# Modulation column sums take a way through DRAM and a turn more before TensorE's product

## The reference, cut to what matters

```python
cs = jax.nn.silu(c)
for i in range(DEPTH):
    ada = cs @ w_ada[i] + b_ada[i]
    sh1, sc1, g1, sh2, sc2, g2 = jnp.split(ada, 6, axis=-1)
    u = x * (1.0 + sc1) + sh1
    ...
    x = _layer_norm(DEEPNORM_ALPHA * x + (1.0 + g1) * y, ...)
```

## Time and profile before

| | |
|---|---|
| median of 3 runs | 3165.83 us (3165.27 to 3168.71) |
| profiled execution, span from first to last instruction | 3166.5 us |
| TensorE busy | 2985.3 us, 94% |
| TensorE weight loads | 2434.7 us, 77% |
| VectorE busy | 1981.5 us, 63% |
| ScalarE busy | 1090.8 us, 34% |
| GpSimd busy | 97.7 us, 3% |
| DMA | 346.08 MB, mean 109 GB/s |
| mean granted TensorE clock | 0.976 |

### The profile page before, as it was taken

The page is one execution under the profiler, slowest core; times in us unless marked ns, Lnnn a source line. Parts: engine busy times, 40 slices in busy tenths (PEclk is TensorE's granted clock), DMA queues, the critical chain, the costliest instruction groups (busy, mean ns, idle before and its releaser), DMA issues.

```text
span 3166.5 us, 45854 instructions
## 1 busy us (share of the span) xinstructions
PE 2985.3 (94%) x19638; PEld 2434.7 (77%) x19656; DVE 1981.5 (63%) x3051; ACT 1090.8 (34%) x1667; POOL 97.7 (3%) x116
## 2 busy tenths in 40 slices
PE   6998999999988999997999999899999998899999
PEld 5876888887865788884867887678887877778887
DVE  5856897787567896787455777654444255554353
ACT  2334432233156332233333333242223244542122
POOL 0000000000000000000002222000000001000000
PEclk8999999999998999998999999899999999999999
DMA  8751554545530464542210000222322220032232
GB/s 235 187 160 54 180 179 163 183 160 173 189 106 21 153 199 146 200 163 65 95 49 11 13 13 10 103 87 97 103 93 92 83 94 27 8 107 93 94 105 81
DMA packets 236543, 346.08 MB, mean 109 GB/s; under 512 B 19620, under 2 KB 121964, under 8 KB 236340
## 3 DMA queue, kind: packets, MB, share of 16 engines
q1 hardware_dynamic: 221236, 329.63, 32.3%
q10 hardware_dynamic: 15104, 13.52, 1.3%
HBM read 340.97 MB, written 2.15 MB: 108 GB/s over the span
## 4 chain that ended last, share of the span: by engine, by line
PE 80%; DVE 11%; ACT 5%; DMA 2%; issue 1%; SPq 0%; DVEq 0%; ACTq 0%
PE bank L141 79%; DVE w_tiles L150 2%; PE bank L144 2%; DVE w_low L150 1%; DMA first_ada<-in_w_ada 1%; ACT w_high L147 1%; DVE ada_acc L162 1%; DMA weight_ring<-in_d_w_in 1%; DVE w_g L150 1%; ACT w_tiles L147 1%; DVE x_natural L162 1%; ACT L147 1%; ACT stage L147 0%; DVE d_sm L168 0%; DVE x_sm L168 0%
## 5 line engine op out<-in xcount | busy, mean ns | idle before, releaser
L150 DVE TENSOR_TENSOR w_low<-weight_ring,w_high 128x2048 fp32r<-128x2048 f32 (+2 forms) x212 | 463.8, 2188 | 450.4 <-ACT w_high L147 450.4
L147 ACT ACTIVATE w_high<-weight_ring 128x2048 fp32r<-128x2048 f32 (+2 forms) x212 | 388.1, 1831 | 610.4 <-DMA weight_ring<-in_mlp_down 178.9
L141 PE MATMUL bank<-u_high,w_high 128*128 128x512 f32 x1472 | 578.4, 393 | 12.1 <-DVE w_low L150 6.2
L141 PE MATMUL bank<-u_high,w_low 128*128 128x512 f32 x1472 | 574.8, 390 | 0.0
L141 PE MATMUL bank<-u_low,w_high 128*128 128x512 f32 x1472 | 574.6, 390 | 0.0
L141 PE MATMUL bank<-w_high,u_high 128*128 128x512 f32 x896 | 353.3, 394 | 6.8 <-DVE w_low L150 2.5
L141 PE MATMUL bank<-w_low,u_high 128*128 128x512 f32 x896 | 351.1, 392 | 0.0
L141 PE MATMUL bank<-w_high,u_low 128*128 128x512 f32 x896 | 351.0, 392 | 0.0
L141 PEld LDWEIGHTS bank<-u_high,w_high 128*128 128x128 f32 x1472 | 277.5, 189 | 70.6 <-ACT stage L147 7.1
L141 PEld LDWEIGHTS bank<-u_high,w_low 128*128 128x128 f32 x1472 | 277.4, 188 | 58.7
L141 PEld LDWEIGHTS bank<-u_low,w_high 128*128 128x128 f32 x1472 | 277.7, 189 | 57.0
(11 more groups left out here) (411 smaller groups left out, 4362.5 us busy)
## 6 DMA issues: line engine op xcount, KB each, us to landing
ada_ring<-in_mod_w SPq DMA_DIRECT2D x48, 1024.0 KB, 7.5
weight_ring<-in_f_w_up SPq DMA_DIRECT2D x44, 1024.0 KB, 5.1
ada_ring<-in_w_ada SPq DMA_DIRECT2D x40, 1024.0 KB, 7.1
weight_ring<-in_mlp_up SPq DMA_DIRECT2D x32, 1024.0 KB, 5.4
weight_ring<-in_mlp_down SPq DMA_DIRECT2D x32, 1024.0 KB, 5.0
weight_ring<-in_f_w_down SPq DMA_DIRECT2D x24, 768.0 KB, 4.7
weight_ring<-in_m_w_in SPq DMA_DIRECT2D x16, 1024.0 KB, 10.2
weight_ring<-in_d_w_in SPq DMA_DIRECT2D x12, 1024.0 KB, 5.3
```

The lines of the kernel that those rows point to most:

```text
L141: return self.e.matmul(out, l, r, start=start, stop=stop, skip_group_check=True)
L147: return self.e.activation(out, in_, f, **kw) if self.live else QUIET
L150: return self.e.tensor_tensor(out, a, b, op) if self.live else QUIET
```

## The change

- VectorE's eight operations on a block stay, but the sum is made in place in `ada_ring`: the second half (s = 1) first, then the first half, whose first operation adds the sum of the second. `ada_acc` and VectorE's wait for the product before it are gone.
- SyncE sends the sum, 128 x 512 floats, to DRAM (`sp_sum_out`) in the block that follows: it issues the half s = 1, waits for the sum, stores it, waits until the store has landed, and issues the half s = 0.
- SyncE loads the sum back (`sp_sum_in`) in another order: 128 floats on each partition, four such groups side by side. In its queue this stands behind the first weight tile of the next turn.
- GpSimd adds the four groups with two additions, of 128 x 256 and 128 x 128 (`pool_sums`).
- TensorE makes one product instead of four, with the 128 x 128 sum as the stationary operand and a 128 x 4 picking matrix as the moving one, a turn later than before (`takes`); so the first turn of m_qk has none and the first turn of g0_up0 has one.
- `pick` is made once by a VectorE reduction at the start.
- The gate f0 is stored and loaded between f0_up0 and f0_dn0 (before: stored in the m cell, loaded at the start of f0). Gates d and x are stored behind dn0 instead of ahead of it, and g1 behind g0_dn0.

```diff
@@ -299,10 +300,10 @@
...
         self.small = take("small", [P, 96])
-        self.fold, self.eps = self.small[:, 64:80], self.small[:, 80:82]
+        self.fold, self.eps, self.pick = self.small[:, 64:80], self.small[:, 80:82], self.small[:, 88:92]
         self.X = take("x_natural", [P, TT, D])
         self.aring = take("ada_ring", [P, 2, 2048])
-        self.aacc = take("ada_acc", [P, 512])
+        self.asum = take("ada_sum", [P, 4, P])
         weights = -(-ar.top // 64) * 64
...
@@ -489,13 +490,16 @@
...
         at = turn = 0
-        self.ada_bank = {}
+        self.takes, summed = {}, None
         for x in lin:
...
             turn += x.turns
-            for i, b in enumerate(x.ada or ()):
-                self.ada_bank[b] = x.group(i)
+            for i, b in enumerate(x.ada):
+                if summed is not None:
+                    self.takes[x.name, i] = summed
+                summed = b
+        self.takes["g0_up0", 0] = summed
         self.lin = {x.name: x for x in lin}
...
@@ -559,6 +563,8 @@
...
             self.sp_weight(sp, w)
+            self.sp_sum_in(sp)
+        self.sp_sum_out(sp, last.ada[-1])
         sp.wait_ge(self.T, "used", last.tile(last.turns - 1, len(last.pieces) - 1))
...
@@ -634,12 +642,44 @@
...
         w = self.ada_blocks[b][0]
-        for s in range(2):
+        for s in (1, 0):
             if b > len(self.ada_first):
-                sp.wait_ge(self.V, "ada used", b - 1, s)
+                if s:
+                    sp.wait_ge(self.V, "ada used", b - 1)
+                else:
+                    self.sp_sum_out(sp, b - 1)
+                    sp.wait_ge(self.fold_out, b - 1)
             src = w[s * 512:(s + 1) * 512, :].rearrange("(k p) n -> p k n", p=P)
...
             sp.dma_start(dst, src).then_inc(*self.ada_in[s].landed(b))
+
+    def sp_sum_out(self, sp, b):
+        if b > self.stored_sum:
+            sp.wait_ge(self.V, "ada summed", b)
+            if b - 2 >= len(self.ada_first):
+                sp.wait_ge(self.fold_in, b - 2)
+            sp.dma_start(self.fold_rows[b % 2], self.aring[:, 0, 0:512]).then_inc(*self.fold_out.landed(b))
+            self.stored_sum = b
+
+    def sp_sum_in(self, sp):
+        b = self.stored_sum
+        if b > self.loaded_sum:
+            sp.wait_ge(self.fold_out, b)
+            if b > len(self.ada_first):
+                sp.wait_ge(self.T, "ada", b - 1)
+            src = self.fold_rows[b % 2].rearrange("a n -> (a n)").rearrange("(q p m) -> p q m", q=4, p=P)
+            sp.dma_start(self.asum[:], src).then_inc(*self.fold_in.landed(b))
+            self.loaded_sum = b
+
+    def pool_sums(self, g, *names):
+        for name in names:
+            for i in range(self.lin[name].turns):
+                if (name, i) in self.takes:
+                    b = self.takes[name, i]
+                    g.wait_ge(self.fold_in, b)
+                    g.tensor_tensor(self.asum[:, 0:2, :], self.asum[:, 0:2, :], self.asum[:, 2:4, :], ALU.add).then_inc(*self.G.up())
+                    g.wait_ge(self.G)
+                    g.tensor_tensor(self.asum[:, 0, :], self.asum[:, 0, :], self.asum[:, 1, :], ALU.add).then_inc(*self.G.up("folded", b))
 
...
@@ -754,43 +793,41 @@
...
                 self.T.mark("used", w)
-            if i < len(L.ada):
-                self.pe_ada(pe, L.ada[i])
+            self.pe_ada(pe, name, i)
             if between and i == 0:
...
 
-    def pe_ada(self, pe, b):
-        bank = self.ada_bank.get(b, 7)
-        pe.wait_ge(self.V, "ada summed", b)
-        if bank in self.free:
-            pe.wait_ge(*self.free[bank])
-        for j in range(4):
-            m = pe.matmul(self.bank[bank][:, j:j + 1], self.aacc[:, j * P:(j + 1) * P], self.ones[:, 0:1], True, True)
-        m.then_inc(*self.T.up("ada", b))
-        self.free[bank] = (self.V, "mod", b)
-
-    def dve_ada_take(self, v, b):
-        _, bias, at, _ = self.ada_blocks[b]
-        v.wait_ge(self.T, "ada", b)
-        v.tensor_tensor(self.mod[:, at:at + 4], self.bank[self.ada_bank.get(b, 7)][:, 0:4], bias, ALU.add).then_inc(
-            *self.V.up("mod", b))
+    def pe_ada(self, pe, name, i):
+        if (name, i) in self.takes:
+            b, bank = self.takes[name, i], self.lin[name].group(i)
+            pe.wait_ge(self.G, "folded", b)
+            if bank in self.free:
+                pe.wait_ge(*self.free[bank])
+            pe.matmul(self.bank[bank][:, 0:4], self.asum[:, 0, :], self.pick, True, True).then_inc(*self.T.up("ada", b))
+            self.free[bank] = (self.V, "mod", b)
+
+    def dve_ada_take(self, v, name, i):
+        if (name, i) in self.takes:
+            b, bank = self.takes[name, i], self.lin[name].group(i)
+            _, bias, at, _ = self.ada_blocks[b]
+            v.wait_ge(self.T, "ada", b)
+            v.tensor_tensor(self.mod[:, at:at + 4], self.bank[bank][:, 0:4], bias, ALU.add).then_inc(*self.V.up("mod", b))
 
...
         cs = self.ada_blocks[b][3]
-        for s in range(2):
+        for s in (1, 0):
             v.wait_ge(self.ada_in[s], b)
+            acc = self.aring[:, s, 0:512]
             for t in range(4):
...
                 src = self.aring[:, s, t * 512:(t + 1) * 512]
-                if s == t == 0:
-                    v.wait_ge(self.V)
-                    if b > len(self.ada_first):
-                        v.wait_ge(self.T, "ada", b - 1)
-                    v.tensor_scalar(self.aacc[:], src, col, None, ALU.mult).then_inc(*self.V.up())
+                v.wait_ge(self.V)
+                if t:
+                    v.scalar_tensor_tensor(acc, src, col, acc, ALU.mult, ALU.add).then_inc(*self.V.up())
+                elif s:
+                    v.tensor_scalar(acc, src, col, None, ALU.mult).then_inc(*self.V.up())
                 else:
-                    v.wait_ge(self.V)
-                    v.scalar_tensor_tensor(self.aacc[:], src, col, self.aacc[:], ALU.mult, ALU.add).then_inc(*self.V.up())
-            self.V.mark("ada used", b, s)
+                    v.scalar_tensor_tensor(acc, src, col, self.aring[:, 1, 0:512], ALU.mult, ALU.add).then_inc(*self.V.up("ada used", b))
         self.V.mark("ada summed", b)
...
@@ -865,8 +902,8 @@
...
                 xs, tmp = self.X[:, t, i * 512:(i + 1) * 512], self.stage[:, t % 2, :]
-                if t == TT - 1 and i < len(L.ada):
-                    self.dve_ada_take(v, L.ada[i])
+                if t == TT - 1:
+                    self.dve_ada_take(v, name, i)
                 v.wait_ge(self.T, "sum", name, i, t)
...
@@ -1162,6 +1199,8 @@
...
         self.dve_split(v, 1)
+        v.wait_ge(self.core_in, "core")
+        v.tensor_reduce(self.pick, self.ident.rearrange("p (r g) -> p g r", g=4), ALU.add).then_inc(*self.V.up("pick"))
 
...
@@ -1241,7 +1280,6 @@
...
         self.act_norm_rows(a, self.m_ln, 0)
-        self.act_gate_store(a, "f0")
         self.act_turn(a, "m o u", self.cols["m_norm_g"], None)
...
@@ -1305,6 +1342,7 @@
...
     def pool_m(self, g):
+        self.pool_sums(g, "m_qk", "m_v", "m_o")
         self.join(g, self.G, "m cell start")
...
@@ -1507,13 +1545,16 @@
...
         f, st = self.f[l], f"f{l}"
-        self.act_gate_load(a, st, f["gb"][:])
+        if l:
+            self.act_gate_load(a, st, f["gb"][:])
         self.act_norm_rows(a, f["ln"], 2 * l + 1)
...
         self.act_ffn_up(a, l, st + "_up0", 0, None)
-        for gate in (("x",) if l else ("d",)):
-            self.act_gate_store(a, gate)
+        if not l:
+            self.act_gate_store(a, "f0")
+            self.act_gate_load(a, "f0", f["gb"][:])
         self.act_residual(a, st + "_dn0")
+        self.act_gate_store(a, "x" if l else "d")
         self.act_ffn_up(a, l, st + "_up1", 6, [(st + "_up0", 10), (st + "_up0", 11)])
...
@@ -1685,6 +1726,7 @@
...
     def pool_diff(self, g):
+        self.pool_sums(g, "m_out", "f0_up0", "f0_dn0", "f0_up1", "f0_dn1", "d_qk", "d_v")
         self.join(g, self.G, "d heads start")
...
@@ -1958,7 +2000,9 @@
...
     def pool_rwkv(self, g):
+        self.pool_sums(g, "d_out", "f1_up0", "f1_dn0", "f1_up1", "f1_dn1", "r_out")
         self.pool_wkv(g)
+        self.pool_sums(g, "g0_up0")
 
...
@@ -2627,6 +2669,8 @@
...
                 self.act_residual(a, f"{st}_dn0")
+                if not l:
+                    self.act_gate_store(a, "g1")
         dn = f"{st}_dn1"
...
@@ -2658,6 +2702,7 @@
...
                         self.dve_ahead(v, up, i, b // 2)
+                self.dve_ada_take(v, up, i)
             if h == 0:
```

More of the change, by code:

```diff
@@ L230, with __init__ @@
 class Net:
-    def __init__(self, nc, ctx, args, out, scratch, gate_rows):
-        self.nc, self.a, self.out, self.scratch, self.gate_rows = nc, args, out, scratch, gate_rows
+    def __init__(self, nc, ctx, args, out, scratch, gate_rows, fold_rows):
+        self.nc, self.a, self.out, self.scratch, self.gate_rows, self.fold_rows = nc, args, out, scratch, gate_rows, fold_rows
         self.T, self.V = Signal(nc, "tensor_done"), Signal(nc, "vector_done")
@@ L515, in write @@
```

(13 more changed lines are left out.)

6 lines of the change are left out of this document (3 added, 3 removed).

## The result

The changed kernel takes 3183.0 us (median of 4 runs, 3178.6 to 3194.3) against 3165.6 us before (4 runs, 3161.7 to 3168.7). The ratio is 1.0058, with a 95% interval from 1.0044 to 1.0072: slower by 0.6%, where 3146 us was forecast. A later session gave 3178.2 us (10 runs) against 3169.0 (20 runs), a ratio of 1.0024 (1.0009 to 1.0038). The profiled execution took 3182.8 us, with a span of 3181.4 us.

The account below looks back on a forecast made before the run. The prediction took TensorE, busy 94% of the span, as the bound. Its terms, 20.5 + 4.4 - 1.6 - 2.7 + 0.4 - 0.8 = 20.2 us off 3165.8, gave 3146 us, range 3129 to 3163.

Parts of the forecast that it names:

- Term 3: SyncE's queue elsewhere: the sum's store delays weight tiles, hidden in dense turns, costing 1.6 us at the end of m_out.
- Term 2: m_o and d_v: TensorE's waits for VectorE's sums go, but later weight tiles limit the gain to 4.4 us.
- Term 5: GpSimd's additions slow VectorE by 0.1 us in each of eight VectorE-set turns, costing 0.8 us.
- Term 4: f0_dn0: gate f0's store and load delay ScalarE and VectorE, so TensorE waits 2.7 us.
- Term 1: Small products on TensorE: six of eight passes go, 0.66 us in 30 turns, 20.5 us with two first turns.
- D: Rival, 10%: sum stores land in 12 us or more, SyncE's tiles come late, dense turns stall; about 3180 us.
- B: Rival, 16%: waits for sums gain nothing, m_out loses 5 us, f0_dn0 8.7 with the clock; about 3159 us.
- E: Rival, 8%: the folded sum is late at the small product, TensorE waits for GpSimd; about 3166 us.
- C: Rival, 10%: GpSimd locks VectorE out for whole instructions in eight turns, 10.4 instead of 0.8 us; about 3155 us.

Follow-up runs that it names:

- e1: The changed kernel measured and profiled once more, with no edit: 3178.2 us.
- e7: The changed kernel with f0's gate rows stored a stage earlier, ahead of f0_up0's passes on ScalarE: 3168.9 us, ratio 0.9984.
- e2: The kernel before with one four-column small product in place of four, leaving out part of the sums; no DRAM, GpSimd or later turn: 3147.4 us, ratio 0.9918.
- e5: The changed kernel with the sum in its own tile and f0's gate rows stored a stage earlier: 3146.1 us, ratio 0.9908.
- e6: The changed kernel without GpSimd's two additions, three of four partial rows left out: 3172.3 us, ratio 0.9987.
- e11: e5 without GpSimd's two additions, three of four partial rows left out: 3139.5 us, ratio 0.9901.
- e12: The kernel before measured and profiled once more, with no edit: 3171.4 us.
- e4: The changed kernel with the sum in its own tile, so the first half loads without waiting for the store's landing: 3159.0 us, ratio 0.9969.
- e3: The kernel before with its four small products a turn later from a second accumulator, gate rows moved, no DRAM or GpSimd: 3165.0 us, ratio 0.9991.

## Why the prediction was wrong

The forecast was 3146, the result 3183, outside the range of 3129 to 3163. At r_r.0 the forecast's terms give -19.7 us and the run gave +4.4. Of these 24 us Term 3 misses 10, Term 2 9, Term 5 4 and Term 4 2, and Term 1 gave 2 more than it promised. By its own steps:

- **Term 1** held: 0.70 us a turn instead of 0.66 and 28 free turns instead of 30, 19.6 us against 19.8. The first turn of m_qk gave 2.1 (1.1 in e1). That m_qk.1 and m_qk.2 were counted among the free turns was wrong: they lost 2.7.
- **Term 2** is -5.0 us where +4.4 stood. Its chain of waits was right: the waits of the earlier trace rows went, 4.5 and 5.0 us, the tile in m_o went out 4.7 us later in its stage where I had 4, and the cell and the heads started 1.6 us sooner, counted from the start of m_o.0 and d_v.0, where 2.3 and 2.1 stood. What failed is what I left out behind it. I saw that VectorE would set the joint start while TensorE's turn got shorter, and put no price on the idle time that this opens, 6.35 and 6.23 us: a lower clock was priced only behind the gap that went away. The cell behind it took 4.4 us longer and the heads 3.8, 8.2 of the 9.4 us that this term misses. For the cell all fourteen traces bear this out, for the heads they don't (first section).
- **Term 3** had the mechanism and not the size, nor the places: 1.6 us for m_out, which lost 3.7 with m_v.0's 5.4 and m_qk's 2.7 besides. The store's landing was taken as 4 us; SyncE waited 5.6 on average and up to 13.0, in m_qk and m_v.0, where the weight tiles of m_w_in land in a median of 11.7 us and those of f_w_up in 5.4. That the dense turns hide the wait was right. SyncE's lead over TensorE is a stock: a wait takes from it, and where tiles land slowly it isn't refilled before the next wait, as the chain into m_v.0 shows. In e1 the chain at that place has only a weight tile that lands in 13.6 us and no wait of SyncE, so how much of m_v.0's 5.4 is the wait and how much the execution is not settled. The estimate of 2.6 us in the prediction, from the Trainium skill, "DMA: Bandwidth & Descriptors", the anatomy of one DMA, is half of the median of 5.2 us; that section describes DMAs that GpSimd issues, and these are SyncE's, with other transfers beside them.
- **Term 4** had mechanism, place and even the wait: forecast 2.7 us, measured 2.83. The gate store landed in 10.2 us (11.4 assumed) but went out 2.5 us into the stage (526.5 against 524.0) where I had 0.4, behind a pass and a split on ScalarE. The agreement of the wait is partly luck, a store 2.1 us later and landing 1.2 us sooner; e1 has 4.0 us. What failed is that I kept the lower clock behind the gap, 3.4 us, for the bad end of the range only. It came (last section), and the term is 5.9 us (e7).
- **Term 5** was 3.3 to 3.6 us instead of 0.8, 0.6 us in each of six turns (the first turn of each up0 was free after all). The growth of 0.3 us in the earlier trace rows for each of two additions would have given that; I took a sixth of it without a row. Another 1.3 us of what the six turns lost against before is not GpSimd's: e2 has it too, with no work for GpSimd, so VectorE-bound turns give back part of what the turn before them saved.
- The **attention stages** were in no term, and this execution lost 10 us there to the lower clock. e5 with the whole change in it lost none, so they are not shown to be the change's.

Of the rivals, D comes nearest in its number (3180) and was right about who does it, SyncE's wait for the store; its condition was wrong: it counts on stalls in the dense turns, which stayed free. At the tails and in m_qk and m_v a landing of 5 to 13 us already tells, so its number is near by luck. B had the kinds right, 5 us for m_out (3.7 measured), 8.7 for f0_dn0 with its clock (5.9) and nothing won in term 2 (-5.0), but nothing for m_qk and m_v. E hardly occurred: e1 has three waits for a folded sum, 1.6 us in all, e7 two, 3.5 us, and this is the only one in the changed kernel's first trace (TensorE's weight loads, in total, times, longest).

```profile
PEld bank L141 <- POOL ada_sum L150: 0.6, 1, 0.6
```

C's price of 10.4 us was too high by a factor of three: e6 and e11 measure 3.3 and 3.6. The rule of the Trainium skill, "SBUF — State Buffer", section "SBUF: two separate sides", that the loser of the shared ports waits for the whole instruction of the other engine, goes with this as follows. The trace of the changed kernel agrees, and in both directions: who starts first decides. Where an addition of 128x256 had started first, f_g<-f_g,f_a took 1.23 us (four times) instead of 0.68, and f_hidden_low 1.11 (twice) instead of 0.69. Where VectorE had started first, neither grew (two and nine times), nor did w_low of 128x2048 at 2.29 (four times), and the addition took the longer: 2.2 and 2.7 us behind two of these w_low instead of 0.74. So an addition costs VectorE some 0.4 to 0.55 us where it comes first and nothing where it comes second or in a gap, which is how 1.3 us of additions a turn cost 0.6.

Corrected by the runs, the sum for e5 is -20.2 us for its 29 free turns, -9.5 for the waits of the earlier trace rows, +3.4 for the m cell behind its gap and +5.1 for the six turns with GpSimd, some -21 us; nothing for gate rows that are stored early nor for a store that nobody waits for. Measured at r_r.0 are -26.0, the rest in turns at joins (m_qk.0 -1.8, d_qk.0 -2.9, d_v.1 -2.2, f1_dn1.1 +1.7, of which e12 has d_qk.0 -2.2 and f1_dn1.1 +1.8 without any edit). That it ends at the forecast's 3146 is partly chance.

The 3.4 us that m_o.1 keeps in e4, e5 and e11 lie in the cell: it starts as early in its turn as before (25.3, 25.6 and 25.2 us against 25.6), but TensorE, done sooner, idles 3.0 to 3.4 us ahead of it, and the cell takes 70.2 to 70.6 us. In e3 nothing of this gap is there, and the cell is at 66.6. No run changes the gap alone, so that it is the cause is the likely reading and not a proof. Here are the product and the cell in e5:

```profile
246.85 0.85 PE L145 MATMUL bank<-core_constants,m_gates 4*128 4x4 f32 x8 [3.42 <-DVE modulation_columns L151]
...
246.80:317.00 70.20, 59.62 (x271) 0.85 0.16 54
```

Still open are what sets the clock in the heads and in the attention stages, and how m_v.0's loss is made up.

## What to carry to other kernels

A wait put into an in-order DMA queue costs whoever stands behind it, and its price is not the landing time at one place but also the lead it takes from later transfers; look first where the lead is already small, and ask whether a tile of its own would make the wait needless. Where a change shortens one engine's turn ahead of a join that another engine sets, it opens a gap there, and the stretch behind that gap belongs into the sum as well. When a change both saves and delays, test the two apart: here 2 KB of tile per partition and a store moved a stage up turned a loss of 0.2 to 0.6% into a gain of 0.9%.

## What the runs showed of the hardware

Code that no kernel here changes ran at different lengths: x_gate.1 at 155.1, 158.3 or 163 to 165 us by trace, at a granted clock of 1.00 in before and 0.94 in the changed kernel, and the wkv turn r_v.1 at 413.3 and 417.7 us in the two traces of before, 414.7 and 426.2 in those of the changed kernel, with 0.96 in the shortest and 0.92 in the longest. The m cell took 66.6 to 67.0 us behind 0.3 to 0.7 us of idle TensorE and 69.5 to 71.3 behind 3.0 to 6.4. A median store of 256 KB landed in 5.2 us and the load of the same 256 KB in 7.9 in the changed kernel (5.5 and 5.8 in e5):

```profile
fold_rows<-ada_ring SPq DMA_DIRECT2D x48, 256.0 KB, 5.2
ada_sum<-fold_rows SPq DMA_DIRECT2D x48, 256.0 KB, 7.9
```

And the gap of 2.8 us in f0_dn0 was followed by 6.8 us at TensorE's lower level (granted clock 0.50, 1.2 instead of 2.4 GHz), which is how it cost 5.9 us in all, against the 32.89 us of the turn in e7:

```profile
543.48 0.80 PE L141 MATMUL bank<-w_high,f_hidden_high 128*128 128x512 f32 x1 [2.83 <-DVE w_low L150]
...
542.70:549.50 6.80, 6.02 (x14) 0.50 0.40 141
```
